# A transformer trunk on one core: first weights of three phases loaded a phase ahead, sums of squares behind the first products, six tiles block by block

## The reference, cut to what matters

```
h = x
for i in range(2):
    n = rmsnorm(h, attn_norm_g[i])
    m = dsa_mixer(n, ...) if i == 0 else chunk_band_mixer(n, ...)
    h = h + m @ w_out[i]
    h = h + conv_ffn(rmsnorm(h, ffn_norm_g[i]), w_up[i], conv_w[i], conv_b[i], w_down[i])
```

## Time and profile before

| what | us |
|---|---|
| median of three runs | 2888.97 (2886.75 to 2891.81) |
| the profiled execution, its own time | 2885.74 |
| its span in the profile | 2884.0 |
| PE busy in it | 2759.1 (96%) |
| DVE, ACT, POOL busy | 1462.7, 1127.2, 834.6 |
| first FFN: barrier, first product | 721.7, 728.8 |
| band phase: barrier, first product | 1462.1, 1475.5 |
| second FFN: barrier, first product | 2143.1, 2150.3 |

### The profile page before, as it was taken

One profiled execution on the slowest core, in us unless ns is written; L12 is line 12 of the kernel. 1 busy time (PEld: TensorE's weight loads), 2 busy tenths in 40 slices (PEclk: granted clock), 3 DMA queues, 4 the chain that ended last, 5 costly groups with the idle time before them and its releaser, 6 DMA issues. The chain is left out here.

```text
span 2884.0 us, 38664 instructions
## 1 busy us (share of the span) xinstructions
PE 2759.1 (96%) x14646; PEld 2375.8 (82%) x14678; DVE 1462.7 (51%) x2412; ACT 1127.2 (39%) x2409; POOL 834.6 (29%) x471
## 2 busy tenths in 40 slices
PE   7799989999999999999989998999989999999999
PEld 6598878887788888888879998888878888888887
DVE  5888656641544444544441115777334445444444
ACT  5676656641422222222244456666323222222221
POOL 2124332102332332233244442111033322323232
PEclk9899999999999999999989999999999999999999
DMA  5110000101211111111031100001011111111111
GB/s 170 45 45 20 7 8 9 63 8 37 75 58 44 44 51 51 44 44 58 15 116 64 45 23 7 27 12 65 23 66 44 57 46 44 46 56 51 44 49 61
DMA packets 38754, 132.43 MB, mean 46 GB/s; under 512 B 4240, under 2 KB 12608, under 8 KB 36960
## 3 DMA queue, kind: packets, MB, share of 16 engines
q1 hardware_dynamic: 38624, 130.68, 13.8%
HBM read 122.22 MB, written 13.69 MB: 47 GB/s over the span
## 5 line engine op out<-in xcount | busy, mean ns | idle before, releaser
L330 PE MATMUL banks<-XH,WH 128*128 128x512 f32 x1408 | 439.8, 394 | 5.4 <-POOL WL L291 4.3
L291 POOL TENSOR_TENSOR WL<-WR,WH 128x1024 fp32r<-128x1024 f32 x132 | 334.1, 2538 | 379.3 <-ACT WH L245 379.3
L330 PE MATMUL banks<-XL,WH 128*128 128x512 f32 x1408 | 440.3, 394 | 0.0
L330 PE MATMUL banks<-XH,WL 128*128 128x512 f32 x1408 | 436.4, 391 | 0.0
L260 ACT ACTIVATE Y<-U,CONVB,CONVW 128x1024 f32<-128x1024 f32 x88 | 109.5, 1245 | 642.5 <-DVE U L386 642.5
L386 DVE TENSOR_TENSOR U<-banks,RB 128x1024 f32<-128x1024 f32 x88 | 107.7, 1224 | 415.4 <-PE banks L330 406.3
L330 PEld LDWEIGHTS banks<-XH,WH 128*128 128x128 f32 x1408 | 265.4, 189 | 63.1 <-POOL WL L291 4.5
L330 PEld LDWEIGHTS banks<-XH,WL 128*128 128x128 f32 x1408 | 265.2, 188 | 60.8
L330 PEld LDWEIGHTS banks<-XL,WH 128*128 128x128 f32 x1408 | 265.6, 189 | 57.9
L376 DVE TENSOR_TENSOR XT<-XT,banks 128x1024 f32<-128x1024 f32 x176 | 214.5, 1219 | 164.5 <-PE banks L346 164.5
L299 POOL TENSOR_TENSOR AL<-Y,AH 128x1024 fp32r<-128x1024 f32 x44 | 106.2, 2415 | 614.4 <-ACT AH L268 614.4
(11 more groups left out here) (237 smaller groups left out, 5317.2 us busy)
## 6 DMA issues: line engine op xcount, KB each, us to landing
WR<-in_ffn SPq DMA_DIRECT2D x132, 512.0 KB, 3.5
QWR<-in_qkv SPq DMA_DIRECT2D x12, 1536.0 KB, 6.5
XT<-in_xT SPq DMA_DIRECT2D x16, 512.0 KB, 7.5
OWR<-in_w_o SPq DMA_DIRECT2D x16, 512.0 KB, 3.4
spill<-XT SPq DMA_DIRECT2D x8, 512.0 KB, 14.0
XT<-spill SPq DMA_DIRECT2D x8, 512.0 KB, 7.9
outT<-XT SPq DMA_DIRECT2D x8, 512.0 KB, 2.6
near<-strip SPq DMA_DIRECT2D x1, 3072.0 KB, 21.1
```

The costliest lines, as they stand in the source:

```text
L291: pool.tensor_tensor(WL[:, ch % RING, :], WR[:, ch % RING, :], WH[:, ch % RING, :].bitcast(F32), ALU.subtract).then_inc(w_lo, 1)
L330: mm = pe.matmul(u[:, h * HALF:(h + 1) * HALF], w[:, ch % RING, db * P:(db + 1) * P], x[:, db, h * HALF:(h + 1) * HALF], start=(db == 0 an ...
```

## The change

- **FFN, first weights.** The first two chunks are no longer loaded in the phase: the attention phase ahead loads them (first attention once all its logits are done, the second behind the reload of `XT`). SP passes their arrival on, then loads the other two of the ring. ACT splits the first `WH` before any `XH` and the second behind block 3.
- **FFN, norm.** DVE joins `ACC` behind two blocks of `XL` and makes `VAR` behind five and `DG` behind seven. PE runs the sums of squares between blocks 2 and 3 of `up(0)`, and spreads `DG` behind block 0 of `up(1)`. POOL's order stays.
- **Band phase, first weights.** Group 0's weights are loaded in the first FFN, once its last convolution is done, and split there by ACT and POOL while PE runs the last down-projection.
- **Band phase, first six tiles.** They go block by block (`project_first`): block db of all six tiles, 18 matmuls, then block db+1. The sums of squares stand ahead of block 3. DVE's order is as in the FFN. The buffers of the weights change places (`slot`), and a few tensors move with them.

```diff
@@ ffn_phase, SP
-            for ch in range(UPC):
+            sp.wait_ge(c.chunks[layer].landed, 16 * EARLY)
+            for ch in range(EARLY):
+                sp.sem_inc(landed[ch], 16)
+            for ch in range(EARLY, UPC):
                 load(None, ch)
...
+            if w_next is not None:
+                sp.wait_ge(convolved, NGRP * UPC)
+                sp.dma_start(c.heads_weights.WR[:], w_next).then_inc(c.heads_weights.landed, 16)
@@ ffn_phase, ACT
+            split_hi(None, 0)
             for db in range(DB):
                 norm.high(act, db)
-                if db in (1, 3):
-                    split_hi(None, db // 2)
+                if db == 3:
+                    split_hi(None, 1)
...
+            if w_next is not None:
+                act.wait_ge(dn_ready, (NGRP - 1) * DB)
+                for h in range(2):
+                    c.heads_weights.high(act, h)
@@ ffn_phase, POOL, behind the last chunk and ahead of the squares
+            if w_next is not None:
+                for h in range(2):
+                    c.heads_weights.low(pool, h)
@@ ffn_phase, PE
                 for db in range(DB):
+                    if n == 0 and db == 3:
+                        norm.tensor(pe)
+                    if n == 1 and db == 1:
+                        spread_factors()
...
-            norm.tensor(pe)
             for n in range(UPC):
                 up(None, n)
-                if n == 0:
-                    pe.wait_ge(diag_ready, 1)
...
@@ ffn_phase, DVE
-            norm.join(dve)
             for db in range(DB):
                 norm.low(dve, db)
-                if db == 2:
+                if db == 1:
+                    norm.join(dve)
+                if db == 4:
                     norm.variance(dve)
-                if db == 5:
+                if db == 6:
                     dve.wait_ge(norm.rstd_ready, 1)
@@ band_phase, SP
-            sp.dma_start(WR[0][:], w_qkv[0]).then_inc(w_landed[0], 16)
-            sp.dma_start(WR[1][:], w_qkv[1]).then_inc(w_landed[1], 16)
+            sp.dma_start(WR[slot(1)][:], w_qkv[1]).then_inc(w_landed[slot(1)], 16)
...
+                    for ch in range(c.chunks[1].count):
+                        sp.dma_start(c.chunks[1].W[:, ch, :], stream[ch]).then_inc(c.chunks[1].landed, 16)
@@ band_phase, ACT
                 norm.high(act, db)
-                if db == 5:
-                    weights_high(0, 0)
-            weights_high(0, 1)
@@ band_phase, POOL
-            weights_low(0, 0)
-            weights_low(0, 1)
@@ band_phase, PE
+            def project_first():
+                pe.wait_ge(first.lows, 2)
+                for db in range(DB):
+                    norm.wait_block(pe, db)
+                    if db == 3:
+                        norm.tensor(pe)
+                    for t in range(len(PJ)):
+                        mm = pass_block(t, db)
+                        if db == DB - 1:
+                            mm.then_inc(pj_ready, 1)
...
-            norm.tensor(pe)
-            for t in range(TILES):
+            project_first()
+            for t in range(len(PJ), TILES):
                 project(t)
@@ band_phase, DVE
-            norm.join(dve)
             for db in range(DB):
                 norm.low(dve, db)
-                if db == 3:
+                if db == 1:
+                    norm.join(dve)
+                if db == 4:
                     norm.variance(dve)
@@ dsa_phase, SP, behind the loads of XT
+            sp.wait_ge(s_ready, ALL)
+            for ch in range(c.chunks[0].count):
+                sp.dma_start(c.chunks[0].W[:, ch, :], stream[ch]).then_inc(c.chunks[0].landed, 16)
```

More of the change, by code:

```diff
@@ L167, in ffn_phase @@
         m = Map(nc, c.scratch, c.end)
-        WR = m.take(f"WR{layer}", [P, RING, D], F32)
+        WR = c.chunks[layer].W
+        m.at += RING * 4 * D
         WH = m.take(f"WH{layer}", [P, RING, D], F32R)
@@ L192, in ffn_phase @@
         AHEAD = 2
+        EARLY = c.chunks[layer].count
         assert CHUNKS == UPC + LOOPS * TURN + PAIRS and TURN % RING == 0
@@ L317, in _, with spread_factors @@
         def _(pe):
+            def spread_factors():
+                pe.wait_ge(diag_ready, 1)
+                for h in range(2):
+                    mm = pe.matmul(c.pair[2][:, h * HALF:(h + 1) * HALF], c.ONES[:],
+                                   DG[:, h * (TT // 2):(h + 1) * (TT // 2), :].rearrange("p t n -> p (t n)"),
+                                   start=True, stop=True)
+                mm.then_inc(spread, 1)
             def up(it, n):
@@ L461, in pieces, with band_phase @@
     return [(a, min(a + HALF, n)) for a in range(0, n, HALF)]
-def band_phase(nc, c, w_qkv, w_o, near, stage, spill):
+def band_phase(nc, c, w_qkv, w_o, near, stage, spill, stream):
     mx = BAND
@@ L482, in band_phase @@
         m = Map(nc, c.scratch, c.top)
[L483 to L486, removed]
+        OH = nc.alloc_sbuf_tensor_at("OWH1", [P, 2, D], F32R, offset=m.at + 2 * 4 * D)
+        OR = nc.alloc_sbuf_tensor_at("OWR1", [P, 2, D], F32, offset=m.at + 4 * 4 * D)
+        OL = nc.alloc_sbuf_tensor_at("OWL1", [P, 2, D], F32R, offset=m.at + 4 * 4 * D)
+        assert c.chunks[1].count * 4 * D <= 2 * 4 * D and 6 * 4 * D <= low_tiles * TILE
         edges = (0, low_tiles, low_tiles + mid_tiles, TILES)
@@ L496, in band_phase @@
         WH, WR, WL = [], [], []
[L497 to L500, removed]
-        XSQ = nc.alloc_sbuf_tensor_at("XSQ1", [P, DB, S], F32, offset=units_at)
[L502 to L506, removed]
+        WH.append(m.take("QWH1", [P, DB, PROJ], F32R))
+        WR.append(nc.alloc_sbuf_tensor_at("QWR1", [P, DB, PROJ], F32, offset=m.at))
+        WL.append(m.take("QWL1", [P, DB, PROJ], F32R))
+        first = c.heads_weights
+        assert m.at == first.at
+        WH.append(first.WH)
+        WR.append(first.WR)
+        WL.append(first.WL)
+        m.at = first.end
+        XSQ = nc.alloc_sbuf_tensor_at("XSQ1", [P, DB, S], F32, offset=units_at)
+        u = Map(nc, units_at, first.at)
+        v = Map(nc, first.at, first.end)
+        KH = [v.take("KH10", [P, 2, S], F32R)]
+        QS = v.take("QS1", [P, 2, S], F32R)
+        DUP = v.take("DUP1", [P, 2, NH * PAIR], F32)
         KH.append(u.take("KH11", [P, 2, S], F32R))
@@ L990, in _, with dsa_phase @@
             squares.add(dve, DB - 1)
-def dsa_phase(nc, c, w_o, near, x):
+def dsa_phase(nc, c, w_o, near, x, stream):
     mx = DSA
@@ L2078, with __init__, half, high @@
     pass
+class FirstChunks:
+    def __init__(self, nc, at, layer):
+        self.count = 2
+        self.W = nc.alloc_sbuf_tensor_at(f"WR{layer}", [P, RING, D], F32, offset=at)
+        self.landed = nc.alloc_semaphore(f"chunks{layer}")
+class HeadsWeights:
+    def __init__(self, nc, at):
+        self.at = at
+        self.WH = nc.alloc_sbuf_tensor_at("QWH1F", [P, DB, PROJ], F32R, offset=at)
+        self.WR = nc.alloc_sbuf_tensor_at("QWR1F", [P, DB, PROJ], F32, offset=at + 4 * DB * PROJ)
+        self.WL = nc.alloc_sbuf_tensor_at("QWL1F", [P, DB, PROJ], F32R, offset=at + 4 * DB * PROJ)
+        self.end = at + 2 * 4 * DB * PROJ
+        self.landed, self.highs, self.lows = (nc.alloc_semaphore(f"heads_w{k}") for k in range(3))
+    def half(self, h):
+        return slice(h * DB // 2, (h + 1) * DB // 2)
+    def high(self, act, h):
+        act.wait_ge(self.landed, 16)
+        act.activation(self.WH[:, self.half(h), :], self.WR[:, self.half(h), :], ACT.Copy).then_inc(self.highs, 1)
+    def low(self, pool, h):
+        pool.wait_ge(self.highs, h + 1)
+        pool.tensor_tensor(self.WL[:, self.half(h), :], self.WR[:, self.half(h), :],
+                           self.WH[:, self.half(h), :].bitcast(F32), ALU.subtract).then_inc(self.lows, 1)
 class FirstHeads:
@@ L2135, in program @@
         c.laid = nc.alloc_semaphore("laid")
+        c.chunks = [FirstChunks(nc, c.scratch, layer) for layer in range(2)]
+        mid_rows = 4 * DB * S // (4 * PROJ)
+        c.heads_weights = HeadsWeights(nc, c.scratch + (BAND.groups * TT - mid_rows) * 4 * PROJ + 2 * 4 * DB * PROJ)
         c.signals = Signals(nc)
```

48 lines of the change are left out of this document (23 added, 25 removed).

## The result

The changed kernel took 2891.56 us (median of 22 runs, 2888.41 to 2898.63) and the kernel before, beside it, 2887.03 (2883.14 to 2891.81). The ratio is 1.0019, 95% interval 1.0013 to 1.0025: 4 to 7 us slower. The profiled execution, at 2896.63, lies at the upper end of its kernel's runs; that of before lay a little under its median. So a part of the 10.8 us between the two spans (2894.8 and 2884.0) is the choice of execution. One run of `xl_first` (7757.62) and one of the kernel before beside it (10017.08) took several times the usual and are left out of the ratios.

A forecast was written before the change was run, and what follows sets the result against it. PE, busy 96% of the span, was taken as the bound. Both FFN starts (+3.4) and the band phase (-0.7) gave +2.7 on the median 2888.97, so 2891.7 us; own range 2888 to 2896, whole range 2884 to 2900.5.

The forecast's parts named there:

- the likeliest case: Whole program: time within 0.2% of the kernel before, chance 0.58.
- +2.7: Whole program: us slower than before, from +3.4 for both FFN starts and -0.7 for the band phase.
- Start of the products: First product 4.7 us behind the barrier in both FFNs and 2.5 in the band phase.
- The `XL` that meets the first split: FFN start: `XL` block 0 meets POOL's first weight split and ends behind it, 4.7 us from the barrier.
- Sums of squares: Moved among the products, they cost PE 1.8 us at full clock at each FFN and band start.
- The chain behind RSTD: Each FFN: `DG` before POOL's second split, PE waits 2.0 us for last `XL`; 0.9 later plus 0.8 clock, +1.7.
- the rival, at 0.28: Both FFNs: POOL's second split before `DG`, PE waits 4.3 us, each start costs 3.5 more; 2898.6 us, chance 0.28.
- that row: Earlier FFN trace: `DG` at 733.43 ran its 1.21 us undisturbed although POOL's split had been issued at 732.59.
- The wait for group 1's weights: Band phase: PE waits 4.2 us before tile 8 and 2.7 within it, 6.9 together.
- The band term, -0.7: Band phase: 9.9 us earlier, less 6.9 waiting for group 1's weights and 2.3 low clock; net -0.7 us.
- The low clock: Behind PE's new waits: 0.8 us each FFN start (bounds 0 and 1.6), 2.3 in the band phase (1.7 to 2.9).
- +3.4: Both FFN starts together: slower by this many us, +1.7 each.

The follow-up runs named there:

- xl_first: The changed kernel, but DVE makes `DG` behind the last `XL` block in both FFNs; 2880.06 us, ratio 0.9975 to the kernel before.
- split_nudge: The changed kernel with a short POOL memset between `RSTD` and the second weight split in both FFNs; 2885.29 us, ratio 0.9995 to the kernel before.
- pool_first: The changed kernel, but DVE waits for POOL's second split before `DG` and its third before the last `XL`, both FFNs; 2893.7 us, ratio 1.0022.
- w1_early: The changed kernel, but group 1's weights are split at the start of the band phase, not behind takes 3 and 4; 2886.38 us, ratio 0.9992.
- sums_first: The changed kernel with the sums of squares ahead of all FFN products again, early chunks and later spreading kept; 2880.05 us, ratio 0.998.
- sums_w1: The changed kernel with the edits of `sums_first` and `w1_early` together; 2875.66 us, ratio 0.9961 to the kernel before, five runs.
- xl_w1: The changed kernel with the edits of `xl_first` and `w1_early` together; 2875.83 us, ratio 0.9958 to the kernel before, five runs.
- dg_first: The changed kernel, but POOL waits for `DG` before its second weight split in both FFNs; 2881.41 us, ratio 0.9982 to the kernel before.

## Why the prediction was right, and where it was not

The time, 2891.56, was forecast as 2891.7, inside 0.2% of before, the likeliest case. The absolute number came out; the change did not quite, and two of the terms of its sum were wrong. The forecast took 0.2% as what a measurement can tell. The 22 runs tell less than 0.1%: the kernel is slower by 4 to 7 us, clear of noise, where +2.7 was forecast.

- **Start of the products.** 4.7 and 2.6 us behind the barrier against 4.7 and 2.5. The `XL` that meets the first split was right.
- **Sums of squares.** 1.84 at full clock, inside the stream, as taken from the earlier trace rows.
- **A reading.** The prediction has the second FFN of before repeat the first within 0.1 us. That holds for the start of `up(1)`, but the wait for `XL` block 7 there was 0.93 us, not 0.22; the low clock at its start was shorter by 1.7. The spreading of before starts at 742.90 in the trace, not at 742.7, and takes 1.3 us; with the block ahead of it the sum comes out the same.
- **The chain behind RSTD, the term that failed.** The forecast had `DG` ahead of the second split, as it was in before, and made it 0.9 plus 0.8 for the clock. What happened is the rival, at 0.28: POOL first, a wait of 4.1 (rival: 4.3), the clock down for 3.4 us behind it. Measured: +4.3 a start, where the forecast had +1.7 and the rival +5.2. The rival's price was too high mainly by its clock: 3.4 us by 0.47 is 1.6, the low end of the 1.6 to 2.9 that it took. Its sum also slips: 3.5 for each start is 7.0, not 6.9, and its own terms (2.3, and the middle of 1.6 to 2.9 less 0.8) make 3.75. `split_nudge` shows that the forecast's numbers were right for the order that it assumed.
- **Why that row misled.** In it DVE was in the middle of a row of `XL` when the split asked. In the changed kernel DVE stands idle at the semaphore, and the split starts 0.06 us ahead. `pool_first` and `split_nudge` show that this order decides the wait. I gave more weight to one row from another situation than to the order of the queues. The Trainium skill, SBUF — State Buffer, section "SBUF: two separate sides", has whichever of the two instructions starts first hold the shared ports for its whole length. The trace agrees here in all six starts of the changed kernel, and in `split_nudge`.
- **The wait for group 1's weights.** Forecast 4.2 and 2.7; measured 3.78 and 1.59 in the first profile, 3.6 to 3.7 and 1.1 in the others. ACT takes tiles back to back every 1.62 us, not 1.75, and the half tile between the waits took 2.95 us and not 2.1, with the clock at 0.5 from 1513.6 on. `w1_early` shows that the wait for these weights is the cause. The band term, -0.7, was mis-sized: -1.9 in the mean, about -1.5 at equal pace.
- **The low clock** behind the waits came as forecast: 3.4 us in the FFNs, 6.8 from 1513.6 in the band phase with the second wait inside. It is not the largest part of what varies between executions of the band phase; the pace of the products is, and the prediction had no term for it.

The net: +8.5 and -1.9 instead of +3.4 and -0.7. By phases that is 4 us more than forecast; the median moved by 4.5 and the ratio says 4 to 7. That the absolute time was hit to 0.1 us is luck. The median of three runs that the forecast started from, 2888.97, lay 1.9 above that of the 22, and the median moved by 1.8 more than forecast; the two errors cancel.

## What to carry to other kernels

When work is moved so that it no longer stands in the way of a start, ask which chain it feeds: here the sums moved behind the products feed `RSTD`, and two engines whose instructions do not run side by side wait for that at the same moment, with the instruction that PE needs last in the row. Put what PE waits for ahead of what can wait (`XL` before `DG`), or hold the other engine back; each of these is one line and turned a loss of 4.3 us a start into a gain of 1.1. And tiles that finish together bring everything behind them late: whatever is done per tile for the next group has to be done before. Then going block by block pays: 672.0 against 675.7 tile by tile; without that it is the slower order.

## What the runs showed of the hardware

- Who runs first behind a common release hangs on 0.3 us: with the split starting 0.06 us before `DG`, `DG` took 3.43; with it 0.19 behind, `DG` took 1.23 and the `XL` behind it 3.41.
- A waiting split does not always go next. In four kernels (before, `sums_first`, `xl_first`, `sums_w1`) a split was issued 0.8 us before a `DG` that stood right behind a row of `XL`, and `DG` ran its 1.21 first, in both FFNs of each. In `xl_w1`, with the same FFN code as `xl_first` and the same 0.83 us, the split went first in both. So neither the order of the instructions nor the kind of `DG` settles it; what does stays open. An `XL` right behind `DG` lost to a waiting split in each case but one (`dg_first`, where the split came 0.16 us behind the `XL`).
- At a granted clock of 1.00 the same 128x384 products ran at three paces, 851, 860 and 867 in 150 us, each kept through an execution. Two executions of the changed kernel differ by it. Compare phases at equal pace.
- A wait of 1.9 us left the clock at full speed (`split_nudge`), one of 4.1 did not: 3.4 us at 1.2 GHz behind it. The gap of 1.66 us in the earlier trace rows had 3.4 us behind it too, so the length of the wait alone does not settle it.
